# Placement in SBUF of the layers' weight buffers, the first layer's x and the gated outputs

## The reference

```python
h = rms_norm(x, norm)
q, k, v, g = projections of h            # layer 2: k and v from a second norm of x
o = attention(q, k, v)                   # layer 1: banded, relative bias; layer 2: decays of a forget gate
x = x + (o * silu(g)) @ w_out
```

## Time and profile before

| | |
|---|---|
| median of 3 runs | 2486.99 us (2485.85 to 2489.94) |
| the profiled execution | 2486.6 us, span 2484.9 us |
| PE busy | 2457.6 us, 99% |
| DVE busy | 1754.9 us, 71% |
| ACT busy | 1219.4 us, 49% |
| HBM read | 437 MB, 177 GB/s over the span |

### The profile page before, as it was taken

The page is one execution under the profiler, slowest core; times in us unless marked ns, Lnnn a source line. Parts: engine busy times, 40 slices in busy tenths (PEclk is TensorE's granted clock), DMA queues, the critical chain, the costliest instruction groups (busy, mean ns, idle before and its releaser), DMA issues.

```text
span 2484.9 us, 43962 instructions
## 1 busy us (share of the span) xinstructions
PE 2457.6 (99%) x16586; PEld 2187.6 (88%) x16586; DVE 1754.9 (71%) x2629; ACT 1219.4 (49%) x1811; POOL 304.0 (12%) x397
## 2 busy tenths in 40 slices
PE   8999999999999999999999999999999999999998
PEld 7999999888888888888888888888888888888887
DVE  8988797996767566666666668667576756666676
ACT  6555333665544444444534456544444444444445
POOL 1212114422100000000000001111010001000011
PEclk9999999999999999999999999999999999999999
DMA  7666763486576666666666665767667766766673
GB/s 216 173 160 170 196 183 87 111 225 189 162 193 187 191 175 181 184 173 193 175 193 186 175 174 167 194 186 185 191 171 190 193 184 182 189 180 181 189 194 102
DMA packets 758308, 442.79 MB, mean 178 GB/s; under 512 B 28784, under 2 KB 721136, under 8 KB 758160
## 3 DMA queue, kind: packets, MB, share of 16 engines
q1 hardware_dynamic: 752880, 430.16, 61.8%
q0 software_dynamic: 5280, 10.56, 3.2%
HBM read 437.35 MB, written 3.31 MB: 177 GB/s over the span
## 4 chain that ended last, share of the span: by engine, by line
PE 95%; DVE 3%; issue 1%; DMA 0%; ACT 0%; POOL 0%; SPq 0%; DVEq 0%; ACTq 0%
PE bank L288 40%; PE bank L294 20%; PE bank L269 5%; PE bank L270 5%; PE bank L271 5%; PE bank L318 5%; PE bank L319 5%; PE bank L320 5%; PE bank L1851 1%; PE bank L1870 1%; PE bank L1858 1%; PE bank L1850 1%; PE bank L1871 1%; DVE lob L253 0%; DMA rawa<-in_w_in_dram 0%
## 5 line engine op out<-in xcount | busy, mean ns | idle before, releaser
L253 DVE TENSOR_TENSOR lob<-rawb,hib 128x1024 fp32r<-128x1024 f32 x672 | 834.6, 1256 | 377.1 <-ACT hib L246 371.0
L246 ACT ACTIVATE hib<-rawb 128x1024 fp32r<-128x1024 f32 x672 | 701.4, 1055 | 515.5 <-PE bank L294 368.0
L288 PE MATMUL bank<-xx,hib 128*128 128x512 f32 x3328 | 842.7, 395 | 0.5 <-DVE xx L2126 0.3
L288 PEld LDWEIGHTS bank<-xx,hib 128*128 128x128 f32 x3328 | 601.5, 189 | 110.5 <-DVE xx L2126 0.9
L294 PEld LDWEIGHTS bank<-xx,lob 128*128 128x128 f32 x3328 | 459.8, 190 | 32.8
L294 PE MATMUL bank<-xx,lob 128*128 128x256 f32 x3328 | 487.3, 285 | 0.0
L269 PE MATMUL bank<-xh,hia 128*128 128x258 f32 (+2 forms) x1040 | 301.7, 290 | 10.7 <-DVE loa L253 10.5
L270 PE MATMUL bank<-xl,hia 128*128 128x258 f32 (+2 forms) x1040 | 296.5, 285 | 0.0
L271 PE MATMUL bank<-xh,loa 128*128 128x258 f32 (+2 forms) x1040 | 295.8, 284 | 0.0
L288 PE MATMUL bank<-oo,hib 128*128 128x512 f32 x1008 | 256.7, 393 | 0.0
L269 PEld LDWEIGHTS bank<-xh,hia 128*128 128x128 f32 x1040 | 197.3, 190 | 15.6 <-DVE loa L253 10.7
(11 more groups left out here) (294 smaller groups left out, 2260.4 us busy)
## 6 DMA issues: line engine op xcount, KB each, us to landing
rawb<-in_a_w_in_dram SPq DMA_DIRECT2D x256, 512.0 KB, 4.7
rawa<-in_w_in_dram SPq DMA_DIRECT2D x130, 512.0 KB, 5.4
rawb<-in_kv_w_dram SPq DMA_DIRECT2D x128, 512.0 KB, 4.5
rawb<-in_b_w_in_dram SPq DMA_DIRECT2D x128, 512.0 KB, 5.2
rawb<-in_a_w_out_dram SPq DMA_DIRECT2D x64, 512.0 KB, 5.1
rawb<-in_b_w_out_dram SPq DMA_DIRECT2D x64, 512.0 KB, 5.0
rawb<-in_w_out_dram SPq DMA_DIRECT2D x32, 512.0 KB, 4.8
table<-in_rel_dram POOLq DMA_DIRECT2D x32, 128.0 KB, 4.0
```

The lines of the kernel that those rows point to most:

```text
L246: nc.scalar.activation(self.hi[(2 * at.u + h) % SPL][:], self.raw_half(at, h), ACT.Copy).then_inc(hi_ready, 1)
L253: nc.vector.tensor_tensor(self.lo[b][:], self.raw_half(at, h), self.hi[b][:].bitcast(F32), ALU.subtract).then_inc(lo_ready, 1)
L288: nc.tensor.matmul(out, self.hi[b][:, k * P:(k + 1) * P], both(k).rearrange("p a t -> p (a t)"), start=start and k == 0, stop=False)
```

## The change

`place_split` gets an argument `apart`: behind each `hi` and `lo` buffer it allocates so many fp32 elements that nothing uses. The layers' stream takes 8, 32 bytes; the first phase's takes none. `spaced` allocates `xx0` with tiles of 2 · 256 + 16 elements and `oo` with 2 · 256 + 8, and returns the view without the added elements: tiles of `xx0` are 2112 bytes apart and those of `oo` 2080. `xx1` stays at 2048. `spare0`, 64 elements or 256 bytes, stands behind `bk` in the first phase, as long as the eight gaps of 32 bytes together.

```diff
-        def place_split(self):
-            self.hi = [sbuf(self.stack, f"hi{self.tag}{i}", [P, HALF], F32R) for i in range(SPL)]
-            self.lo = [sbuf(self.stack, f"lo{self.tag}{i}", [P, HALF], F32R) for i in range(SPL)]
+        def place_split(self, apart=0):
+            self.hi, self.lo = [], []
+            for kept, name in ((self.hi, "hi"), (self.lo, "lo")):
+                for i in range(SPL):
+                    kept.append(sbuf(self.stack, f"{name}{self.tag}{i}", [P, HALF], F32R))
+                    if apart:
+                        sbuf(self.stack, f"apart_{name}{self.tag}{i}", [P, apart])
...
     bk = sbuf(first, "bk", [P, CT, 2, LP])
+    spare = sbuf(first, "spare0", [P, 64])
     vv = sbuf(first, "vv", [P, CT, LP])
...
     st = Stream(ph, "b", 4, U_WOUT)
-    st.place_split()
+    st.place_split(8)
     xx1 = sbuf(ph, "xx1", [P, KT, 2, SEQ], F32R)
     st.place_raw()
     x1 = sbuf(ph, "x1", [P, KT, SEQ])
-    xx = [sbuf(ph, "xx0", [P, KT, 2, SEQ], F32R), xx1]
+    def spaced(name, tiles, apart):
+        t = sbuf(ph, name, [P, tiles, 2 * SEQ + apart], F32R)
+        return t[:, :, 0:2 * SEQ].rearrange("p k (a t) -> p k a t", a=2)
+    xx = [spaced("xx0", KT, 16), xx1]
...
-    oo = sbuf(ph, "oo", [P, GH, 2, SEQ], F32R)
+    oo = spaced("oo", GH, 8)
```

## The result

The changed kernel takes 2501.35 us, the kernel before 2486.78 us on the same chip: ratio 1.0059, interval 1.0047 to 1.0071. It is slower by 14.6 us, and the forecast was 2461. The profiled execution has a span of 2499.0 us, 14.1 us over that of before.

The account below looks back on a forecast made before the run. The prediction took PE's time per matmul as the bound. Gains of 16.8 and 3.2 us on L288, 3.7 on L294 and 2.3 on L318 to L320 made 26 us, from 2486.6 to 2461 us; range 2415 to 2497.

Parts of the forecast that it names:

- What bounds the kernel: PE, busy 99% at 2.4 GHz with almost no waits in the layers, so only time per matmul could change.
- The hypothesis: Reads of the moving tile and of the next weights disturb each other by placement, explaining 13 to 18 ns per matmul.
- The rule: TensorE has two independent SBUF read ports, so placement would have no say and time would stay at 2487.
- the sum: Layers' matmuls: L288 16.8 us on xx0 and oo, 3.2 on xx1; L294 3.7; L318 to L320 2.3; together 26 us gained.
- The 1 to 3 ns: First phase's 256-wide matmuls, walking through remainders, were read as about this much below the layers' common remainder.
- The slower rival: In the layers' 512-wide runs, changing address relations stop runs settling, 12 us each on L288 and L318 to L320: 2511; chance 0.13.
- half price: Half of the slower rival's loss in the layers' 512-wide matmuls, giving 2499 us.
- The bound of the large gain: All the layers' matmuls at plain fp32's lower overhead, 130 us gained, 2356; the large-gain rival had chance 0.13.
- The edits costed at nothing: spare0's shift, the hi and lo splits and the loads: no cost expected, a 5% slower split hidden by idle time.

Follow-up runs that it names:

- lo 32 below: Kernel before the change, with hi buffers at the moving tiles' remainder and lo buffers 32 bytes below it modulo 256: 2490.39 us against 2488.61, ratio 1.0008.
- the longer tiles: Changed kernel without gaps behind the weights' buffers, only tiles of xx0 (2112 bytes) and oo (2080) longer: 2497.81 us against 2486.51 for the kernel before.
- the control: Changed kernel with spare0 kept, the 256 bytes in one piece before xx1, tiles at 2048 bytes again: 2486.37 us against 2486.51 for the kernel before.
- the last kernel: Tiles of xx1 and oo 64 bytes above the weights' remainder, xx0 at it: 2481.40 us against 2487.51 for the kernel before, ratio 0.9977.

## Why the prediction was wrong

- **What bounds the kernel** held: PE's time per matmul moved and nothing else did, and the sum of the forms' differences, 14.0 us, is the difference of the spans, 14.1, but for 0.1.
- **The hypothesis** that a matmul's time depends on where both operands lie held too. The rule that the prediction quoted against it, from the Trainium skill's "TensorE: Matmul & The Clock Gate", Part 2, does not fit the rows: with the instructions, their order and their sizes the same, moving the weights' buffers from 64 to 96 bytes below the tiles took the time from 3.5 us under the kernel before to 28.1 us over it, in one execution each (1.8 under and 29.1 over by the forms' sums). What the two reads share isn't shown.
- **The step that failed** is the one in the sum that took "the first phase's 12 ns of overhead as what a walk through remainders leaves, at either width, because the overhead comes with the load of 128 columns of weights". For 256 columns it was near: L298 (the former L294) went from 118.9 to 117.8 and 118.0 by starts on `xx`, as forecast, but stayed at 118.9 on `oo`. That was partly luck. The 1 to 3 ns were read from mean durations, and the layers' mean of 285 holds matmuls with others put between them; by starts the first phase's three lines take 117.0, 119.0 and 119.0, only 0.6 ns less than the layers. For 512 columns it was wrong in sign. They were at 230.1 and, settled, at 227; the walk took them to 232.1 on `xx0`, 232.7 on `xx1` and 232.4 on `oo`, where 225.5, 228.5 and 225.5 were forecast. The turned form was at 227 and went to 231.3, 233.2 and 232.6; 225.5 was forecast. No row of before had 512 columns at another distance than zero, and I filled that with the narrower rows; zero was one of the two best distances for 512 columns in the wide form, as the table shows.
- **The slower rival** had the right sign, the right places and about the right size (2499 to 2511), and a mechanism of which a part holds. Changes of the distance do disturb, as lo 32 below and the longer tiles show. But a constant distance of 32 bytes costs 13.6 us where the change costs 14.6, with no change of distance inside a run, so runs whose distance walks are not needed for the loss. The sign that the prediction named for this rival, that the turned form rises, came; it comes at a constant 32 bytes too (233.3), so it doesn't tell the two apart. The range ended at 2497 and left out even this rival's half price, 2499.
- **The bound of the large gain**, 130 us, was nowhere near: in no kernel did the mean of the wide form's 512 columns on a tile come under 229.3 ns, that of the turned form under 226.5 or that of 256 columns under 114.1, while the plain fp32 matmuls of 256 and 128 columns, with as many steps, start 215 to 218 and 109 to 113 ns apart in the trace of before. What is left between them stays open.
- **The edits costed at nothing** were: `spare0` (the control), the loads, and the splits, which stayed at 1056 and 1241 ns against the earlier trace rows:

```profile
L257 DVE TENSOR_TENSOR lob<-rawb,hib 128x1024 fp32r<-128x1024 f32 x634 | 778.2, 1241 | 380.1 <-ACT hib L250 375.0
...
L250 ACT ACTIVATE hib<-rawb 128x1024 fp32r<-128x1024 f32 x633 | 661.1, 1056 | 506.7 <-PE bank L298 356.4 <-PE bank L324 149.6
```

Why a distance is good or bad, and why 64 above is the best for 256 columns and one of the poor ones for 512 in the wide form, was not settled; the runs give the table and no circuit.

## What to carry to other kernels

In a dense stretch of F32R matmuls with 128 columns of weights loaded beside each, the placement of the two in SBUF modulo 256 bytes was worth some nanoseconds per matmul, from 2481 to 2517 us in all; measure it at each width that the kernel uses, as the sign can differ between them, and price no width from another. Set the distance by whole tiles and runs, not within a run. Where buffers have happened to lie at one common remainder, that is a setting like any other and can be among the good ones.

## What the runs showed of the hardware

- On fp32r operands, with 128 columns of weights loaded beside each matmul, start to start is 227 ns for 512 columns at distance zero when settled and 233 at 32 bytes; for 256 columns it is 120 and 117. A shift by 256 bytes changes nothing; 32, 64, 96 and 128 bytes do.
- Which side is which counts and not the names: streaming 64 bytes above what is loaded gives 226, 229, 232 in turn in the wide and in the turned form, and streaming 64 bytes below it gives, in both, 231 and 236 in turn or a steady 233 to 234.
- Several settled states exist at one distance. With the weights 64 below, runs on `oo` are at 113 ns throughout in buffers 1 and 3 and at 117 to 118 in buffers 0 and 2, though all four lie at the same remainder. It isn't the buffer: in the last kernel, at the same distance, 0 and 2 are at 114 and 1 and 3 at 117 to 118. What ran before is the difference that I can see.
